# Stick-breaking attention in pairs of blocks: scores, sigmoids, selects, transposes and products with v two blocks at a time

## The reference

```python
def one_block(args):
    i, q_blk = args
    z = jnp.einsum('bhqd,bhkd->bhqk', q_blk, kt).astype(jnp.float32) * scale
    q_pos = i * BLOCK + jnp.arange(BLOCK)
    causal = key_pos[None, :] < q_pos[:, None]
    log_one_minus = jnp.where(causal, jax.nn.log_sigmoid(-z), 0.0)
    suffix = lax.cumsum(log_one_minus, axis=3, reverse=True) - log_one_minus
    log_a = jax.nn.log_sigmoid(z) + suffix
    a = jnp.where(causal, jnp.exp(log_a), 0.0)
    return jnp.einsum('bhqk,bhkd->bhqd', a.astype(vt.dtype), vt)
```

## Time and profile before

| | |
|---|---|
| median of 3 runs | 1041.02 us (1040.95 to 1041.47) |
| the profiled execution | 1040.96 us, its span 1039.2 us |
| busy | TensorE 1028.9 us (99%), VectorE 779.8 (75%), ScalarE 612.0 (59%), GpSimd 43.1 (4%) |
| granted TensorE clock | 0.999 of 2.4 GHz, mean |
| chain that ended last | TensorE 91%, VectorE 6%, ScalarE 1% |

### The profile page before, as it was taken

The page is one execution under the profiler, slowest core; times in us unless marked ns, Lnnn a source line. Parts: engine busy times, 40 slices in busy tenths (PEclk is TensorE's granted clock), DMA queues, the critical chain, the costliest instruction groups (busy, mean ns, idle before and its releaser), DMA issues.

```text
span 1039.2 us, 15629 instructions
## 1 busy us (share of the span) xinstructions
PE 1028.9 (99%) x5916; PEld 880.5 (85%) x5916; DVE 779.8 (75%) x1117; ACT 612.0 (59%) x949; POOL 43.1 (4%) x86
## 2 busy tenths in 40 slices
PE   9999999999999999999999999999999999999997
PEld 8877888888888877788888888998899978888886
DVE  6977678987887887779978887855655677655654
ACT  6667766665656778757656667535443656444442
POOL 1000010000000000100000000501000000000000
PEclk9999999999999999999999999999999999999999
DMA  8643445665555441547655555654443355565541
GB/s 303 231 131 122 130 158 199 204 201 192 187 187 181 147 160 44 180 136 230 203 190 194 181 190 175 199 168 155 153 138 123 122 182 189 179 213 189 175 147 42
DMA packets 114641, 177.44 MB, mean 171 GB/s; under 512 B 3419, under 2 KB 85652, under 8 KB 114580
## 3 DMA queue, kind: packets, MB, share of 16 engines
q1 hardware_dynamic: 113460, 174.26, 50.8%
q10 hardware_dynamic: 1120, 2.36, 0.6%
HBM read 175.56 MB, written 1.05 MB: 170 GB/s over the span
## 4 chain that ended last, share of the span: by engine, by line
PE 91%; DVE 6%; ACT 1%; issue 0%; DMA 0%; POOL 0%; POOLq 0%; SPq 0%; ACTq 0%; DVEq 0%
PE ps L1896 87%; DVE wlo L1208 3%; PE ps L2004 1%; PE ps L2417 1%; PE ps L2050 1%; DVE h L1266 0%; DVE scr L1389 0%; PE ps L2542 0%; DVE scr L1378 0%; DVE scr L1373 0%; ACT whi L638 0%; PE ps L2488 0%; PE ps L2169 0%; DVE scr L1396 0%; DMA scr<-in_attn_norm 0%
## 5 line engine op out<-in xcount | busy, mean ns | idle before, releaser
L1208 DVE TENSOR_TENSOR wlo<-raw,whi 128x2048 fp32r<-128x2048 f32 x148 | 337.8, 2287 | 56.1 <-ACT whi L638 55.9
L1896 PE MATMUL ps<-xs,whi 128*128 128x512 f32 (+1 forms) x1536 | 336.2, 352 | 0.0
L1896 PEld LDWEIGHTS ps<-xs,whi 128*128 128x128 f32 x1536 | 267.4, 189 | 39.6 <-issue 1.7
L638 ACT ACTIVATE whi<-raw 128x2048 fp32r<-128x2048 f32 x148 | 281.0, 1909 | 25.0 <-PE ps L1896 14.9
L1896 PE MATMUL ps<-xs,wlo 128*128 128x256 f32 x1248 | 202.4, 283 | 0.0
L1896 PE MATMUL ps<-whi,xs 128*128 128x512 f32 (+1 forms) x576 | 182.2, 393 | 0.2 <-DVE xs L1798 0.2
L1896 PEld LDWEIGHTS ps<-xs,wlo 128*128 128x128 f32 x1248 | 175.2, 192 | 2.9
L1896 PEld LDWEIGHTS ps<-whi,xs 128*128 128x128 f32 x576 | 107.2, 189 | 23.2 <-issue 2.6
L1896 PE MATMUL ps<-whi,ohi 128*128 128x512 f32 (+1 forms) x370 | 125.4, 397 | 0.0
L1896 PE MATMUL ps<-whi,olo 128*128 128x512 f32 (+1 forms) x370 | 122.5, 389 | 0.0
L1896 PE MATMUL ps<-wlo,ohi 128*128 128x512 f32 (+1 forms) x370 | 122.4, 389 | 0.0
(11 more groups left out here) (189 smaller groups left out, 972.3 us busy)
## 6 DMA issues: line engine op xcount, KB each, us to landing
raw<-in_ffn_w_up SPq DMA_DIRECT2D x44, 1024.0 KB, 5.1
raw<-in_w_in SPq DMA_DIRECT2D x23, 1024.0 KB, 5.3
raw<-in_ffn_w_down SPq DMA_DIRECT2D x22, 1024.0 KB, 4.9
raw<-in_w_mlp_in SPq DMA_DIRECT2D x16, 1024.0 KB, 5.4
raw<-in_w_mlp_out SPq DMA_DIRECT2D x16, 1024.0 KB, 4.9
raw<-in_diff_w_qkv SPq DMA_DIRECT2D x11, 1024.0 KB, 5.3
raw<-in_ple_w_gate SPq DMA_DIRECT2D x8, 1024.0 KB, 4.9
raw<-in_swa_w_qkv SPq DMA_DIRECT2D x6, 1024.0 KB, 5.4
```

What stands on the lines that cost most here:

```text
L638: act.activation(whi[:, u % RING, :], raw[:, u % RAW, :], ACT.Copy).then_inc(hi_ready, 1)
L1208: dve.tensor_tensor(wlo[:, u % RING, :], raw[:, u % RAW, :], whi[:, u % RING, :].bitcast(F32), ALU.subtract).then_inc(lo_ready, 1)
L1896: return pe.matmul(o, l, r, start=start, stop=stop, skip_group_check=True)
```

## The change

Blocks are taken in pairs (`SB_PAIRS`: heads of `pr` and `pr + 1`, same query block), four of them instead of eight. Sigmoids, selects, the product, the high and low parts each handle a pair in one instruction; the running products stay one per head and block. A pair with qt = 1 has 8 transposes, in two groups of 4. TensorE's order becomes: scores 0 in piece 5, piece 6; then for s = 1 to 3 product with v of s-2, first transposes of s-1, scores of s, pieces 5 + 2s and 6 + 2s (for s = 3 the second transposes of pair 2 between pieces 11 and 12); then product with v of pair 2, first transposes of pair 3, piece 13 with the second transposes in its middle, product with v of pair 3. `sbp` and `sbm` move to `xn`, `sbc` to the end of `pp`, `sba` and `ETs` double in size.

```diff
-        sbp = region(0, 512)
-        sbm = region(512, 512)
-        sbc = region(9728, 2 * (SEQ + 1), "p (j c) -> p j c", j=2)
-        sba = region(1024, 512)
-        ETs = region(1536, 512)
+        sbp = xn[:, 0, :]
+        sbm = xn[:, 1, :]
+        sbc = pp.rearrange("p t c -> p (t c)")[:, 2 * D - 4 * (SEQ + 1):2 * D].rearrange("p (j c) -> p j c", j=4)
+        sba = region(0, 1024)
+        ETs = region(1024, 1024)
...
-        SB_BLOCKS = [(pr, qt) for qt in range(2) for pr in range(4)]
+        SB_PAIRS = [(pr, qt) for qt in range(2) for pr in (0, 2)]
...
# ScalarE
-                for s in range(9):
-                    if s > 1:
-                        sb_hi(s - 2)
-                    if s:
-                        sb_copy(s - 1)
-                    if s < 8:
-                        sb_sigmoids(s)
-                    ahead(IN2[5 + s][2])
-                sb_hi(7)
+                sb_sigmoids(0)
+                ahead(IN2[5][2])
+                ahead(IN2[6][2])
+                for s in range(1, 4):
+                    if s > 1:
+                        sb_hi(s - 2)
+                    sb_copy(s - 1, 0)
+                    sb_sigmoids(s)
+                    ahead(IN2[5 + 2 * s][2])
+                    if s == 3:
+                        sb_copy(2, 1)
+                    ahead(IN2[6 + 2 * s][2])
+                sb_hi(2)
+                sb_copy(3, 0)
+                ahead(IN2[13][2])
+                sb_copy(3, 1)
+                sb_hi(3)
...
# VectorE
                 def sb_block(s):
...
-                    for j in range(2):
+                    for j in range(4):
                         ins = dve.tensor_tensor_scan(sbc[:, j, SEQ - nk:SEQ][:, ::-1], sbm[:, j * nk:(j + 1) * nk][:, ::-1],
                                                      ones[:, 0:nk], 1.0, ALU.mult, ALU.mult)
                     settle(ins)
-                    pair = lambda v: v[:, 0:2 * nk].rearrange("p (j c) -> p j c", j=2)
+                    if s == 3:
+                        dve.wait_ge(t_ready, T_USE["2S21"] + 1)
+                    pair = lambda v: v[:, 0:4 * nk].rearrange("p (j c) -> p j c", j=4)
...
-                for s in range(9):
-                    if s < 8:
+                dve.wait_ge(in2_read, in2_count[0])
+                settle(dve.tensor_copy(sbc[:, :, SEQ:SEQ + 1], ones[:, 0:4].unsqueeze(2)))
+                for s in range(4):
+                    n = 5 + 2 * s
+                    ahead(IN2[n][2])
+                    if s < 3:
                         sb_block(s)
-                    ahead(IN2[5 + s][2])
-                    in2_evac(5 + s)
+                        in2_evac(n)
+                        ahead(IN2[n + 1][2])
+                    else:
+                        in2_evac(n)
+                        ahead(IN2[n + 1][2])
+                        sb_block(s)
+                    in2_evac(n + 1)
                     if s:
                         sb_lo(s - 1)
+                ahead(IN2[13][2])
+                in2_evac(13)
+                sb_lo(3)
...
# TensorE
-                for s in range(9):
-                    if s:
-                        weights_T_sb(s - 1)
-                    if 0 < s < 8:
-                        scores_sb(s)
-                    in2(5 + s, None if s else first_scores)
-                    if s:
-                        pv_sb(s - 1)
+                in2(5, first_scores)
+                in2(6)
+                for s in range(1, 4):
+                    if s > 1:
+                        pv_sb(s - 2)
+                    weights_T_sb(s - 1, 0)
+                    scores_sb(s)
+                    in2(5 + 2 * s)
+                    if s == 3:
+                        weights_T_sb(2, 1)
+                    in2(6 + 2 * s)
+                pv_sb(2)
+                weights_T_sb(3, 0)
+                in2(13, lambda: weights_T_sb(3, 1))
+                pv_sb(3)
```

More of the change, by code:

```diff
@@ L397, in three_layer_kernel @@
                 T_ORDER.append(f"1q1{(s - 5) // 2}")
-        T_ORDER += [f"2S{s}" for s in range(8)]
+        for s, (pr, qt) in enumerate(SB_PAIRS):
+            T_ORDER += [f"2S{s}{n}" for n in range(qt + 1)]
         for s, (j, qt) in enumerate(DIL_BLOCKS):
@@ L607, in _ @@
                     pool.tensor_scalar(diag[:, t, :], ident, rboth[:, t:t + 1], None, ALU.mult).then_inc(diag_ready, 1)
-                for s, (pr, qt) in enumerate(SB_BLOCKS):
+                for s, (pr, qt) in enumerate(SB_PAIRS):
                     nk = P * (qt + 1)
@@ L612, in _ @@
                     for buf, fill in ((sbm, 1.0), (sbp, 0.0)):
-                        v = buf[:, 0:2 * nk].rearrange("p (j c) -> p j c", j=2)[:, :, nk - P:nk]
+                        v = buf[:, 0:4 * nk].rearrange("p (j c) -> p j c", j=4)[:, :, nk - P:nk]
                         pool.affine_select(out=v, in_=v, compare_op=ALU.is_gt, fill=fill, base=0,
-                                           pattern=[[0, 2], [-1, P]], channel_multiplier=1).then_inc(sb_sel, 1)
+                                           pattern=[[0, 4], [-1, P]], channel_multiplier=1).then_inc(sb_sel, 1)
                 norm_rstd(7)
@@ L1061, in sb_sigmoids, with sb_copy @@
                 def sb_sigmoids(s):
-                    pr, qt = SB_BLOCKS[s]
+                    pr, qt = SB_PAIRS[s]
                     nk = P * (qt + 1)
-                    act.wait_ge(s_ready, S_AT["S"] + s + 1)
+                    act.wait_ge(s_ready, S_AT["S"] + 2 * s + 2)
                     for buf, sign in ((sbm, -1.0), (sbp, 1.0)):
-                        ins = act.activation(buf[:, 0:2 * nk].rearrange("p (j c) -> p j c", j=2), ps[:, 6:8, 0:nk],
+                        ins = act.activation(buf[:, 0:4 * nk].rearrange("p (j c) -> p j c", j=2), ps[:, 6:8, 0:2 * nk],
                                              ACT.Sigmoid, scale=sign)
                     ins.then_inc(sb_l, 1)
[L1071 to L1074, removed]
+                def sb_copy(s, part):
+                    copy_T(ETs[:, part * HALF:(part + 1) * HALF], ps[:, TB, :])
                 def sb_hi(s):
-                    pr, qt = SB_BLOCKS[s]
-                    act.wait_ge(o_ready, S_AT["S"] + s + 1)
-                    act.activation(ohi[:, pr, qt * P:(qt + 1) * P], ps[:, OB, 0:P], ACT.Copy).then_inc(sb_hi_ready, 1)
+                    pr, qt = SB_PAIRS[s]
+                    act.wait_ge(o_ready, S_AT["S"] + 2 * s + 2)
+                    act.activation(ohi[:, pr:pr + 2, qt * P:(qt + 1) * P], ps[:, OB, 0:2 * P].rearrange("p (a c) -> p a c", c=P),
+                                   ACT.Copy).then_inc(sb_hi_ready, 1)
                 def dil_exp(s):
@@ L1727, in sb_block @@
                     settle(ins)
-                    pair = lambda v: v[:, 0:2 * nk].rearrange("p (j c) -> p j c", j=2)
+                    if s == 3:
+                        dve.wait_ge(t_ready, T_USE["2S21"] + 1)
+                    pair = lambda v: v[:, 0:4 * nk].rearrange("p (j c) -> p j c", j=4)
                     dve.tensor_tensor(pair(sba), pair(sbp), sbc[:, :, SEQ - nk + 1:SEQ + 1], ALU.mult).then_inc(mix_ready, 1)
                 def sb_lo(s):
-                    pr, qt = SB_BLOCKS[s]
+                    pr, qt = SB_PAIRS[s]
                     cols = slice(qt * P, (qt + 1) * P)
                     dve.wait_ge(sb_hi_ready, s + 1)
-                    dve.tensor_tensor(olo[:, pr, cols], ps[:, OB, 0:P], ohi[:, pr, cols].bitcast(F32), ALU.subtract)\
-                        .then_inc(o_read, 1)
+                    dve.tensor_tensor(olo[:, pr:pr + 2, cols], ps[:, OB, 0:2 * P].rearrange("p (a c) -> p a c", c=P),
+                                      ohi[:, pr:pr + 2, cols].bitcast(F32), ALU.subtract).then_inc(o_read, 2)
                 def dil_max(s):
@@ L1757, in dil_out @@
                                       ALU.mult).then_inc(o_read, 1)
-                settle(dve.tensor_copy(sbc[:, :, SEQ:SEQ + 1], ones[:, 0:2].unsqueeze(2)))
                 ahead(IN2[1][2])
@@ L2475, in scores_sb @@
                 def scores_sb(s):
-                    pr, qt = SB_BLOCKS[s]
+                    pr, qt = SB_PAIRS[s]
                     nk = P * (qt + 1)
[L2478 to L2485, removed]
+                    for a in range(2):
+                        for j in range(2):
+                            rows_ = slice(j * HD, (j + 1) * HD)
+                            ins = mm(ps[:, 6 + j, a * nk:(a + 1) * nk], qTb[rows_, pr + a, qt * P:(qt + 1) * P], kTb[rows_, pr + a, 0:nk],
+                                     True, True)
@@ L2486, in weights_T_sb @@
+                    ins.then_inc(s_ready, 2)
+                def weights_T_sb(s, part):
+                    t_begin(f"2S{s}{part}")
                     pe.wait_ge(mix_ready, 16 + s + 1)
-                    for n in range(2 * (qt + 1)):
-                        ins = pe.transpose(ps[:, TB, n * P:(n + 1) * P], sba[:, n * P:(n + 1) * P], ident)
+                    for n in range(4):
+                        c = part * HALF + n * P
```

(13 more changed lines are left out.)

## The result

| | before | changed |
|---|---|---|
| median (7 runs each) | 1040.98 us (1040.6 to 1041.66) | 1044.51 us (1043.88 to 1044.96) |
| the profiled execution | 1040.96, span 1039.2 | 1044.51, span 1042.6 |
| mean granted TensorE clock, profiled execution | 0.999 | 0.995 |

The account below looks back on a forecast made before the run. TensorE, busy 99% of the span, was taken to bound the kernel. A new wait of 4.1 us less 2.5 us saved by merging made 1.6 us more, 1042.6 us, with a range of 1040.3 to 1044.9.

Parts of the forecast that it names:

- the likeliest case: Whole kernel: 4.1 us of new wait less 2.5 us saved, giving 1042.6 us; 55%, own range 1041.6 to 1043.8.
- the first rival: TensorE's clock falls in the pause before pair 3's transposes, costing 2.4 us more: 1045.0 us; chance 12%.
- the one on the clock: Sign of being wrong: matmuls behind the pause come 0.24 us apart, where 0.12 was expected.
- saved by merging: TensorE's products with v, transposes and scores in pairs, with fewer entries and restarts: 2.5 us less, bounds 0.6 to 3.8.
- pause before T(3,0): TensorE waits for VectorE's product before pair 3's first transposes: 4.0 to 4.1 us, bounds 3.0 to 4.6.
- T(3,0) due / product ready, from S: From the start of pair 2's second transposes: pair 3's first transposes due at 7.4 us, VectorE's product ready at 11.4.
- pairs 0 to 2: Their products are ready before TensorE's transposes, with 1.1 us to spare for pair 0 and 1.4 for pair 2.
- work behind the pause: TensorE's matmuls after the wait for pair 3's product: granted clock unchanged, 0.12 us apart.
- The rival "no pause": Pair 3's product is ready when its transposes are due and the 2.5 us stay: 1038.5 us; chance 12%.
- second late product: Rival: another product is late, pair 0's or through selects costing several times more: 1043.5 to 1044.5 us; chance 8%.
- nothing is given back later: Rival: later waits for ScalarE and VectorE return the pause; half returned gives 1040.5 us; chance 5%.
- the bound of 4 us lost in the 8 at the low level: Kernel start: 8 us at 1.2 GHz cost 4 too many, so a clock fall costs between nothing and that.

Follow-up runs that it names:

- e1: The changed kernel with pair 3's scans and product put before the two weight subtractions on VectorE: 1038.53 us, ratio to the kernel before 0.9976.
- e3: The changed kernel with 60 extra matmuls of zeros on TensorE before the first transposes of pair 3: 1042.57 us, ratio to the kernel before 1.0013.
- e6: e1 with the scores of pair 1 taken apart, one head pair before projection piece 7, the other in its middle: 1038.92 us, one run.
- e2: The changed kernel with one weight subtraction before pair 3's scans and one behind its product: 1040.39 us, ratio to the kernel before 0.9993.
- e4: The kernel before, single blocks, with block 7's scans and product put behind the two weight subtractions on VectorE: 1045.98 us, ratio 1.0046.
- e7: The changed kernel with the first half of gate piece 13 before pair 3's first transposes, the second transposes behind its second half: 1040.34 us, ratio to before 0.9994.
- e5: The changed kernel with 30 matmuls of zeros in TensorE's pause, held until the second weight subtraction ended: 1042.48 us, ratio to the kernel before 1.0014.

## Why the prediction was right and wrong

The measured time lies in the range, but by luck: the likeliest case, 1042.6, was not what happened. What happened was the first rival, the clock that falls in the pause, given 1045.0 and 12%, and the range was said to leave out most of it. Of the signs of being wrong, the one on the clock came true: the matmuls after the pause are 0.21 apart.

| step | predicted | measured |
|---|---|---|
| saved by merging | 2.5 us | 2.4 in the time (e1 against before): 2.9 off the stream, 0.4 given back |
| pause before T(3,0) | 4.0 to 4.1 | 3.95 idle; 4.0 by e3 against e1 (1042.57 - 1038.53); the predicted steps add up to 3.97, the 4.1 came of rounding |
| T(3,0) due / product ready, from S | 7.4 / 11.4 | 7.3 / 11.2 (S = 732.70; ready 743.86) |
| pairs 0 to 2 | no wait | none in the trace |
| work behind the pause | at full speed (55%); 2.4 extra (12%) | 1.9 extra by medians, 2.4 in the profile |

- **Merging.** Right for products and scores: 0.59, 0.64, 1.06 and 1.03 against 0.59, 0.64, 1.07 and 1.03. Two of the merged sizes came from another place of the same trace, where a piece of that form stood; the 0.64 was an estimate from them. e6 shows for the scores that being together is what pays. The sum took too little for the transposes that stand directly behind projection matmuls, three groups of four. It gave each an entry of 0.09, and they have none (743.85 to 743.97 in e1 is the usual 0.12). And each is 0.06 shorter than it took: with the two matmuls behind them four took 0.67 (743.97 to 744.64 in e1), not 0.73, and T(0,0) took 0.53, not 0.59. Three times 0.15 is 0.45, and 2.46 + 0.45 = 2.9, as the traces have it. That 2.4 stands so close to 2.5 is partly luck, since the wait at 830 took 0.4 back.
- **The pause.** Right in mechanism and size. e1 removes it with VectorE's order alone, e2 halves it by one of the two subtractions, e4 makes one without pairs. The rival "no pause" named the right lever and had no ground in this kernel.
- **The clock.** This step failed. The sum held only the waits, and the text counted against the rival that a wait of 1.04 us had done nothing. That row bears on 1 us, not on 4. With no row between, even odds for the clock would have been fair, and the likeliest time near 1044 to 1045. The granted clock of 0.55 from 744 to 750, and 1.00 after, is what the trace shows. The rule cited from the Trainium skill, "TensorE: Matmul & The Clock Gate" (Part 1: The HAM clock gate), that an idle TensorE is put back to half clock and must be kept busy to leave it, agrees with it. The price, 2.4, was taken past the middle of a wide bound and came out right partly by luck; the bound is looked at below.
- **The rest.** No second late product, selects hidden (two of 512 columns took 1.23 at 709.93, one 0.61, inside the bound of 0.42 to 0.85). Of the pause nothing is given back later: e3 keeps all of the 4.0 us.

The price of the first rival rests on the bound of 4 us lost in the 8 at the low level at the kernel's start, and the traces do not bear such a loss out. The level there was not the same in each execution, in code that is the same. Eight transposes of the kernel before and of the changed one:

```profile
5.31 1.97 PE L2004 MATMUL ps<-tab,h 128*128 128x128 f32 x8
```

```profile
5.28 1.10 PE L2025 MATMUL ps<-tab,h 128*128 128x128 f32 x8
```

The kernel before worked slowly until about 10, the changed one no longer at 5.3. Yet the changed one was only 0.4 us ahead at its first long wait (52.28 against 52.68). In between it waited for subtractions that the kernel before did not wait for (0.50 at 7.97, 0.53 at 10.97).

The terms for the medians are -2.4 + 4.0 + 1.9 = 3.5, and 1040.98 + 3.5 = 1044.5. They are differences between the same four medians, so they have to add up; what supports them from outside is the traces, 3.95 us of idle time and a slow stretch of 2.4. In the profiled executions the slow stretch costs 2.4 (5.76 against 3.34) while the spans of the changed kernel and e3 differ by 1.8. The changed one was 0.5 us ahead at its first long wait, at 52.28 instead of 52.75, in code that is the same. Of this 0.3 is there by 12 us (the same transposes at 12.02 and 12.33): in e3 the first load is used 0.17 later (5.27 against 5.10), and TensorE waits 0.27 for a cast at 10.04, which it does not in the changed kernel. The rest isn't explained by any run.

## What to carry to other kernels

Merging small pieces on an engine that is never idle pays their fixed parts, here 2.9 us over four pairs, of which 2.4 reached the kernel's time, but a wider batch is worth it only if the engine that feeds it does the batch's work before its bulk work: one swap of two calls on VectorE turned +3.5 us into -2.4. When a stage is regrouped, count from each wait's release what stands ahead of the releasing instruction on its engine, at the piece that is twice as long as the others above all. For a pause that can't be removed, two remedies worked here: own work moved ahead of the wait (e7, 4.2 us better) and empty work in its middle (e5, 2.0 us better).

## What the runs showed of the hardware

- Unbroken idle stretches of TensorE of 0.88, 1.74 and 1.85 us left the granted clock at 2.4 GHz; 2.98 and 3.95 us let it fall to 1.2 GHz, some 2.1 and 2.5 us after their starts. No run has a pause between 1.85 and 2.98 us. A pause of 4 us with 1.85 us of matmuls in its middle kept the upper level.
- After the fall TensorE worked 5.4 us at the low level in the changed kernel's profile and 6.0 in e4's, matmuls of 256 columns 0.21 us apart instead of 0.12. In the changed kernel this cost 1.9 to 2.4 us, about half of what the pause itself cost.
- On the page the fall left a mean clock of 0.995 against 0.999 and, in the row of 40 slices, a single 8 among the 9s (730 to 756 us); a table of stages showed where it began and ended.
- The clock column does not show the low level at the start: it reads 1.00 for the first 14 us of the kernel before, where two matmuls of 512 columns take 1.05 and later 0.62. There the durations have to be read.
